# Masked, scaled scores and their maximum in one accumulating VectorE instruction per query tile, with an additive mask

## What is computed

```python
# dilated window attention: 3 patterns x 16 heads (first block, layer 0)
scores = einsum(q, k) * Dh ** -0.5
mask = (dist >= 0) & (dist <= span) & (kj >= 0)      # causal, windowed, strided
scores = where(mask, scores, -inf)                    # then softmax over keys, times v
# causal attention with a shared rotary key: 16 heads (first block, layer 1)
s = (einsum(qn, kn) + einsum(qp, kp)) * (128 + 64) ** -0.5
s = where(kpos <= qpos, s, -inf);  p = softmax(s);  o = einsum(p, v)
# differential attention: 4 heads of 2 softmaxes, in each of 2 layers (second block)
s = einsum(q, k) * D ** -0.5
s = where(key_idx <= q_idx, s, -inf);  p = softmax(s)
a = p[:, :, 0] - lam * p[:, :, 1];     out = einsum(a, v)
```

## Time and profile before

| what | value |
|---|---|
| median of the runs | 2554.61 us |
| span of the profiled execution, first to last instruction | 2553.1 us |
| what lies around a span (median of the runs less this span) | 1.5 us |
| PE busy | 2513.7 us, 98% |
| DVE busy | 1935.9 us, 76% |
| ACT busy | 1223.6 us, 48% |
| mean granted TensorE clock | 0.999 |
| mean share of the 16 DMA engines, first 1000 us and then | 0.7 to 0.8, then 0.4 to 0.5 |

### The profile page before, as it was taken

One profiled execution on the slowest core, in us unless ns is written; L12 is line 12 of the kernel. 1 busy time (PEld: TensorE's weight loads), 2 busy tenths in 40 slices (PEclk: granted clock), 3 DMA queues, 4 the chain that ended last, 5 costly groups with the idle time before them and its releaser, 6 DMA issues.

```text
span 2553.1 us, 33576 instructions
## 1 busy us (share of the span) xinstructions
PE 2513.7 (98%) x12735; PEld 2109.3 (83%) x12735; DVE 1935.9 (76%) x3285; ACT 1223.6 (48%) x1808; POOL 15.1 (1%) x32
## 2 busy tenths in 40 slices
PE   8999999999999999999999999999999999999999
PEld 6888888888888888878888869888788798888777
DVE  7888988998899888676555647666986667668875
ACT  4444444444444444445555446453455565434553
POOL 0000000000000000000000000000000000000000
PEclk9999999999999999999999999999999999999999
DMA  8787777777787867545445445444445544444444
GB/s 307 257 294 268 277 255 284 280 272 273 247 292 267 299 228 279 202 162 185 142 136 177 157 116 179 150 141 138 143 158 182 176 150 150 134 133 157 153 161 139
DMA packets 266016, 516.95 MB, mean 202 GB/s; under 512 B 16576, under 2 KB 20992, under 8 KB 265216
## 3 DMA queue, kind: packets, MB, share of 16 engines
q1 hardware_dynamic: 264256, 508.43, 58.4%
q0 software_dynamic: 1600, 6.38, 1.0%
HBM read 512.68 MB, written 2.10 MB: 202 GB/s over the span
## 4 chain that ended last, share of the span: by engine, by line
PE 87%; DVE 8%; ACT 3%; issue 2%; DMA 0%; DVEq 0%; SPq 0%; ACTq 0%
PE proj L572 15%; PE proj L574 14%; PE proj L573 14%; PE proj L1223 7%; PE proj L1225 7%; PE proj L1224 7%; PE scores L702 3%; DVE w_lo L1836 2%; PE proj L1215 1%; PE proj L1217 1%; PE proj L1218 1%; PE proj L612 1%; DVE arena L1962 1%; PE proj L613 1%; PE proj L614 1%
## 5 line engine op out<-in xcount | busy, mean ns | idle before, releaser
L1836 DVE TENSOR_TENSOR w_lo<-w_raw,w_hi 128x1024 fp32r<-128x1024 f32 (+1 forms) x740 | 895.2, 1218 | 297.4 <-ACT w_hi L1264 238.7
L1264 ACT ACTIVATE w_hi<-w_raw 128x1024 fp32r<-128x1024 f32 (+1 forms) x740 | 772.9, 1052 | 625.1 <-PE proj L574 374.3
L572 PE MATMUL proj<-w_hi,xt_lo 128*128 128x512 f32 x1632 | 650.9, 399 | 4.1 <-DVE xt_lo L1850 4.0
L574 PE MATMUL proj<-w_hi,xt_hi 128*128 128x512 f32 x1632 | 637.8, 391 | 0.0
L573 PE MATMUL proj<-w_lo,xt_hi 128*128 128x512 f32 x1632 | 636.6, 390 | 0.0
L1223 PE MATMUL proj<-w_hi,xt_lo 128*128 128x512 f32 x976 | 395.5, 405 | 3.5 <-DVE w_lo L1836 3.5
L1225 PE MATMUL proj<-w_hi,xt_hi 128*128 128x512 f32 x976 | 380.9, 390 | 0.0
L1224 PE MATMUL proj<-w_lo,xt_hi 128*128 128x512 f32 x976 | 380.5, 390 | 0.0
L572 PEld LDWEIGHTS proj<-w_hi,xt_lo 128*128 128x128 f32 x1632 | 307.3, 188 | 67.1 <-DVE xt_lo L1850 5.7
L574 PEld LDWEIGHTS proj<-w_hi,xt_hi 128*128 128x128 f32 x1632 | 306.9, 188 | 65.5
L573 PEld LDWEIGHTS proj<-w_lo,xt_hi 128*128 128x128 f32 x1632 | 307.5, 188 | 60.3
(11 more groups left out here) (402 smaller groups left out, 2812.4 us busy)
## 6 DMA issues: line engine op xcount, KB each, us to landing
w_raw<-in_dsa_w_in_dram SPq DMA_DIRECT2D x159, 1024.0 KB, 7.3
w_raw<-in_w_in_dram SPq DMA_DIRECT2D x120, 1024.0 KB, 5.1
arena<-in_w_ada_dram SPq DMA_DIRECT2D x192, 512.0 KB, 5.9
w_raw<-in_w_out_dram SPq DMA_DIRECT2D x32, 1024.0 KB, 5.1
w_raw<-in_mla_w_in_dram SPq DMA_DIRECT2D x24, 1024.0 KB, 5.1
w_raw<-in_dsa_w_out_dram SPq DMA_DIRECT2D x16, 1024.0 KB, 5.1
w_raw<-in_mla_w_out_dram SPq DMA_DIRECT2D x16, 1024.0 KB, 5.1
w_raw<-in_mla_w_ukv_dram SPq DMA_DIRECT2D x8, 1024.0 KB, 5.6
```

What stands on the lines that cost most here:

```text
L572: mm(o, xt[1][:, k0 + kk, tok], WH[:, c % 2, k, 0:n], start=first, stop=False)
L574: ins = mm(o, xt[0][:, k0 + kk, tok], WH[:, c % 2, k, 0:n], start=False, stop=last)
L1264: A(hi[:, 2 * q:2 * q + 2, 0:n], RAW[:, c % 4, 2 * q:2 * q + 2, 0:n], ACT.Copy).then_inc(hi_made, 1)
L1836: V.tensor_tensor(lo[:, ks, 0:n], RAW[:, c % 4, ks, 0:n], hi[:, ks, 0:n].bitcast(F32), ALU.subtract).then_inc(lo_made, 1)
```

## The change

The mask table holds 0 where a key may be seen and -3e38 where it may not (before: +3e38 and -3e38). The mask is added before the scaling, where before it was applied by a minimum after it. One accumulating instruction per query tile writes the masked, scaled scores and leaves their maximum in the engine's accumulator, from where it is written to `MX`; the two separate reductions and the wait between them and the masking are gone.

```diff
-            c[:, at:at + (t + 1) * P] = np.where(ok, BIG, -BIG)
+            c[:, at:at + (t + 1) * P] = np.where(ok, 0.0, -BIG)
...
                 dve.wait_ge(scored, 1 + n + 1)
                 dve.wait_ge(exped, n + 1)
-                own(V.scalar_tensor_tensor(out=SM[:, par, :], in0=SP[:, 0:384], scalar=scale,
-                                           in1=CST[:, K_MASK + 384 * mask:K_MASK + 384 * mask + 384],
-                                           op0=ALU.mult, op1=ALU.min))
-                own.sync()
-                own(V.tensor_reduce(MX[:, h, 0:1], SM[:, par, 0:128], AX_X, ALU.max))
-                own(V.tensor_reduce(MX[:, h, 1:2], SM[:, par, 128:384], AX_X, ALU.max))
+                for t, (a, b) in enumerate(((0, 128), (128, 384))):
+                    at = K_MASK + 384 * mask
+                    own(V.tensor_tensor_reduce(out=SM[:, par, a:b], in0=SP[:, a:b], in1=CST[:, at + a:at + b], scale=scale,
+                                               scalar=-BIG, op0=ALU.add, op1=ALU.max, accum_out=MX[:, h, t:t + 1]))
                 own.sync()
                 if prev is None:
                     V.tensor_scalar(neg, MX[:, h, :], -1.0, None, ALU.mult).then_inc(max_found, 1)
```

## The result

The changed kernel takes 2549.66 us (median of 9 runs, 2548.09 to 2554.57), the kernel before beside it 2555.04 us (9 runs, 2554.49 to 2559.53). The ratio is 0.9976, with a 95% interval of 0.9967 to 0.9986: 5.4 us less, 0.24%. The profiled execution has a span of 2548.4 us and a time of 2550.5, so 2.1 us lie around its span, where I had taken 1.5. The 31 executions of the kernel before that stand beside the change in the first experiment have 2.1 to 2.2 us as well; the 1.5 had set the median of three executions against the span of one that, by this, took about 0.5 us longer. By spans the change is worth 2553.1 - 2548.4 = 4.7 us; my sum said 2.5.

The account below looks back on a forecast made before the run. PE was taken as the bound, busy 2513.7 of 2553.1 us. Six blocks saving 0.42 us each gave 2.5 us less: span 2550.6, plus 1.5 around it, forecast 2552.1 us, range 2550.2 to 2555.6.

Parts of the forecast that it names:

- my sum: Differential attention's first passes: two layers with three blocks of maxima each, 0.42 us saved per block, 2.5 us less.
- the four waits of the first passes: PE waits for the maximum twice per layer in the differential attention, 5.5 us together; ceiling of the gain 6.1 us.
- rival 1: The fused pass on DVE runs at half rate: block 1.18 us, gain only 0.4 us, 2554.2 us; chance 0.16.
- The size of a block: DVE's two passes and two accumulator reads per block of maxima: 0.82 us instead of 1.24, bounds 0.64 to 1.16.
- The other 74 blocks are worth nothing, because PE covers them.: Blocks in dilated attention, layer 1 and second passes: no gain, DVE merely relieved of 31 us and idle for it.
- ACT's exponentials start earlier by the same amount and then wait for PE's turns or for the next half: At those 74 blocks, ACT's earlier start, 0.42 us per block, was to bring PE nothing.
- Rival 3: Dilated attention: DVE's relief also removes PE's two waits for `w_ada` columns, 1.5 us; 4.0 us less, 2550.6; chance 0.07.
- Rival 2's price: Block longer by d costs 10d - 0.3 us in the differential attention's passes; chance 0.07 beyond the bound, 0.05 small loss.
- the dilated attention would still cover it: Dilated attention: four longer blocks add 2.6 us to one of twelve windows, in which DVE idles for 7.9.
- the crossing to a seen loss: Differential attention's passes: the loss passes 5.1 us from a block 0.54 us longer, that is 1.78 us.
- The bound of the gain: A gain over 5.1 us needs a 0.39 us block at the four waits, less than two overlapped passes' 0.53; chance 0.04.
- The 1.5 us around the span: Whole kernel: the median time was taken as 1.5 us above the profiled span, turning 2550.6 into 2552.1 us.

Follow-up runs that it names:

- the first experiment: The change itself measured again, beside its parts on the same chip, against the kernel before: 2549.60 us against 2555.84, ratio 0.9978.
- everywhere else: Fused instruction only in the 64 heads of the dilated attention and layer 1, against the kernel before: 2554.99 us against 2555.84, ratio 0.9992.

## Why the prediction failed by a little

**What held.** PE is the bound, and the four waits of the first passes are the main place. The first of each pair goes, the second shrinks. The block's saving counts three times per layer, and the blocks of the second pass and of the dilated attention, forty-eight heads, bring no shorter wait for the maximum. The passes are as long as the reductions of the same width; rival 1, half rate, would have needed 0.12 us more per 128 columns, and its 1.18 us block did not come.

**The size of a block.** This is the term that was mis-sized. The step "I put the first read at 0.09 ... and the last at 0.17 + 0.03" was too dear: the reads cost 0.00 and 0.12 in sequence, and the block is 0.68 instead of 0.82. Six blocks of 0.56 are 3.4 us; the four waits gave 3.3. This is 0.8 us of the miss. ACT's pair in the earlier trace rows was the wrong neighbour for it: there the next instruction starts 0.09 behind the read, on DVE it starts with it. The Trainium skill's rule (VectorE: DVE Perf Modes, Rules for kernel authors) that one should bring down the number of instructions and not look for gains in fusing does not agree with this trace: four instructions take 0.68 us where three took 1.24, since half of the columns are swept and a read between two passes is free.

**"The other 74 blocks are worth nothing, because PE covers them."** This is the step that failed. For L702's waits it was right. But I had looked only for waits for the maximum, and the maximum also releases ACT, which has a table load and two evacuations to do ahead of PE's next operand. In layer 1 that chain ended 0.3 to 0.6 us late three times, twice at ACT's copy and once behind it at DVE's products: 1.2 us. My sentence "ACT's exponentials start earlier by the same amount and then wait for PE's turns or for the next half" holds only where ACT is ahead of PE. The fusion in layer 1 alone shows the three steps by themselves.

**Rival 3** (relief reaches L746) has the right place and a wrong reason. In the profile PE's wait there at 725 us is 0.4 shorter (0.36 instead of 0.70), but not because DVE got there relieved: it waits for PE at L1989 as the earlier trace rows show, and after the change it waits there just as long (1.3 us). What differs is a pause of DVE before `w_lo`, 0.60 in the kernel before and 0.25 after:

```profile
697.60 1.22 DVE L1836 TENSOR_TENSOR w_lo<-w_raw,w_hi 128x1024 fp32r<-128x1024 f32 x1 [0.60 <-DVE arena L1866]
```

```profile
696.93 1.23 DVE L1836 TENSOR_TENSOR w_lo<-w_raw,w_hi 128x1024 fp32r<-128x1024 f32 x1 [0.25 <-DVE arena L1866]
```

The step is there in every kernel that fuses in the dilated attention (the change twice, everywhere else, with the end of the linear attention later, and with the two reductions kept) and in none that does not. In the kernel with the reductions kept the blocks are longer than before, and the pause is short all the same:

```profile
697.96 1.23 DVE L1836 TENSOR_TENSOR w_lo<-w_raw,w_hi 128x1024 fp32r<-128x1024 f32 x1 [0.25 <-DVE arena L1866]
```

So the 0.4 comes with the change but not from a shorter block or a relieved DVE. The traces show where such pauses fall. Number DVE's records (one for each instruction that the trace lists) from 0, those of its sequencer included: this `w_lo` is record 1599 in the six kernels that have the pause, and 1631 in the change, 1695 with the reductions kept. All 28 pauses of 0.57 to 0.63 us before an instruction that DVE itself had released, in the thirteen profiles together, stand at a record whose number is a multiple of 64 or one less (1599 = 25 x 64 - 1). The 0.61 before a third maximum, with the fusion in the differential attention only, is one of them (4159). Most such numbers have no pause, and what makes it isn't shown. But its place goes with the number of instructions ahead of it, which the change alters.

**Rival 2's price** was wrong by a factor of four, and with it "the dilated attention would still cover it". It compared 2.6 us of added work with 7.9 us of idle time per window, a mean, where the head at 240 us has 0.9 us of slack at its own turn. For the passes of the differential attention the rule itself was about right. I had put the crossing to a seen loss at a block 0.54 longer; at 0.59 longer the loss was 21.7 us.

**The bound of the gain.** "A gain over 5.1 us would need a block of 0.39 us at the four waits alone" left 0.04 of chance. The four waits alone never gave that. They gave 3.3, layer 1 1.2 and L746 0.4, and what brings the medians to 5.4 lies in the spread of the executions. Only L746 was among my cases (rival 3), and for another reason. The 1.5 us around the span was wrong too: it set a median against the span of another execution. With 2.1 us my span of 2550.6 would have given 2552.7, further off.

**How far this is settled.** The parts 3.3 and 1.2 are shown, each by a kernel that has it alone. The 0.4 at L746 is seen and goes with a pause whose place depends on the number of instructions; it is luck of placement, and the cause of the pause is open. The stretches at half clock are seen in single profiles and agree with the spread of the runs. That the change makes them rarer is a matter of counts: none of 31 runs of before has a mean clock of 1.000, but 4 of 9 of the change beside them, 3 of 11 fused in the differential attention only and 4 of 10 fused in its first passes only. That it does so by removing waits of PE is not shown, and one count speaks against it: of the 11 runs with the end of the linear attention later, where all four waits are gone, none has 1.000. So of the 5.4 to 6.2 us by medians, 4.9 have a place in the order of the work (0.4 of it by luck), and the rest stays open.

## What to carry to other kernels

A faster step on an engine that is not the bound is worth what it takes off the waits of the one that is; count at that engine's late starts, and follow from the step each engine that it releases, not only the one that waits for it directly. Where such a wait stands in an order written by hand, first look at what stands ahead of it without a reader: moving some 4 us of such work per layer brought 7.3 us here, more than the better instruction. Judge cover by the slack at each place, never by the mean idle time of a stretch.

## What the runs showed of the hardware beyond that

- A fused pass (add, scale, maximum into an accumulator) with a PSUM and an SBUF source in fp32 takes 291 ns for 128 columns and 420 for 256, and its read of the accumulator 83 ns. That read is free in front of another pass and costs 0.12 us in front of an instruction that waits for it.
- The granted clock falls to half for 3.4 us behind some waits of PE, not at the same places in each execution of one kernel (the change at 1119 and 2034 us in one profile and, up to its last 3 us, nowhere in another). At 2037.9 us of the kernel before, PE had just waited for 1.33 and 1.90 us. It costs 1.5 to 1.7 us where PE has work, and 0.4 at 1119 us, where a wait of PE takes up the rest. With the block masked twice, stretches of 6.8 and 10.2 us occur too.
- All 28 pauses of DVE of 0.57 to 0.63 us behind its own instructions stand at a multiple of 64, or one short of it, in the count of its records. A change of the number of instructions moves them, and with them up to 0.4 us of another engine's wait.
- A loss of PE of up to about 0.2 us behind a matmul doesn't show as idle time, since the modelled ends of matmuls cover it. Comparing the starts of the same matmuls in two traces finds it.
